# Norm and token shift in two parts behind the first MLP, and the weights' low parts there by VectorE, in a two-layer backbone

## What is computed

```python
def rms_norm(x, g, eps=NORM_EPS):
    xf = x.astype(jnp.float32)
    y = xf * lax.rsqrt(jnp.mean(xf * xf, axis=-1, keepdims=True) + eps)
    return (y * g.astype(jnp.float32)).astype(x.dtype)

def modulate(u, shift, scale):
    return u * (1 + scale) + shift

def sq_relu_mlp(u, w_up, w_down):
    return jnp.square(jax.nn.relu(u @ w_up)) @ w_down

def centred_shift(u):
    prev = jnp.pad(u[:, :-1], ((0, 0), (1, 0), (0, 0)))
    nxt = jnp.pad(u[:, 1:], ((0, 0), (0, 1), (0, 0)))
    return 0.5 * (prev + nxt)

# in rwkv_side, for the context and for the latent tokens apart:
    xx = centred_shift(u) - u
    mix = lambda i: u + xx * mu[i]
    xw, xk, xv, xa = mix(1), mix(2), mix(3), mix(4)
    k = xk @ w_rkv[1]
    v = xv @ w_rkv[2]
```

## Time and profile before

| | |
|---|---|
| median of three runs | 2558.79 us (2558.71 to 2562.51) |
| the profiled execution's own time | 2559.15 us |
| its span | 2557.4 us |
| TensorE busy | 2312.6 us, 90% |
| VectorE, ScalarE, GpSimd busy | 43%, 35%, 29% |
| mean granted clock of TensorE | 0.967 |

### The profile page before, as it was taken

How to read it: one execution, slowest core, us unless ns; L and a number is a source line. 1 busy time by engine, 2 the same in 40 slices (tenths; PEclk the granted TensorE clock), 3 DMA queues, 4 the chain that set the end, 5 groups by cost and what they waited for, 6 DMA issues and landing times.

```text
span 2557.4 us, 65184 instructions
## 1 busy us (share of the span) xinstructions
PE 2312.6 (90%) x27579; PEld 1915.4 (75%) x27579; DVE 1103.1 (43%) x2374; ACT 900.8 (35%) x1581; POOL 736.9 (29%) x531
## 2 busy tenths in 40 slices
PE   5998899999999999789978888888988868899998
PEld 3776677888888888668846777777777757888887
DVE  2326666351111212253354666666666644511113
ACT  3555555342121212222223344244244213522324
POOL 0334555232222222353302121121121112344442
PEclk9999999999999999889989999999999978999999
DMA  7125555112222112113410000000000002233321
GB/s 243 50 50 162 169 175 157 50 50 66 66 66 66 66 49 66 49 58 116 136 45 23 12 14 23 12 15 22 12 14 23 4 19 83 83 99 98 98 82 67
DMA packets 172312, 176.31 MB, mean 69 GB/s; under 512 B 26512, under 2 KB 160032, under 8 KB 172064
## 3 DMA queue, kind: packets, MB, share of 16 engines
q1 hardware_dynamic: 172064, 172.62, 21.4%
HBM read 161.06 MB, written 11.53 MB: 67 GB/s over the span
## 4 chain that ended last, share of the span: by engine, by line
PE 81%; DVE 9%; issue 4%; ACT 3%; POOL 1%; DMA 1%; SPq 0%; ACTq 0%; DVEq 0%; PEldq 0%
PE PS L385 39%; PE PS L1386 5%; PE PS L554 4%; PE PS L405 3%; PE PS L738 2%; PE PS L1371 2%; PE PS L1497 2%; PE PS L719 2%; PE PS L1192 2%; PE PS L1361 2%; PE PS L698 2%; PE PS L728 1%; PE PS L1476 1%; PE PS L1046 1%; PE PS L1488 1%
## 5 line engine op out<-in xcount | busy, mean ns | idle before, releaser
L365 POOL TENSOR_TENSOR WL<-RAW,WH 128x1024 fp32r<-128x1024 f32 x178 | 427.6, 2424 | 938.7 <-ACT WH L352 895.6
L385 PE MATMUL PS<-AH,WH 128*128 128x512 f32 (+1 forms) x1024 | 363.8, 355 | 6.2 <-DVE AL L2178 2.4
L385 PE MATMUL PS<-AH,WL 128*128 128x512 f32 (+1 forms) x1024 | 364.2, 356 | 0.0
L385 PE MATMUL PS<-AL,WH 128*128 128x512 f32 (+1 forms) x1024 | 361.6, 353 | 0.0
L352 ACT ACTIVATE WH<-RAW 128x1024 fp32r<-128x1024 f32 x172 | 171.9, 1047 | 271.4 <-PE PS L385 265.7
L385 PE MATMUL PS<-BH,WL 128*128 128x256 f32 (+1 forms) x736 | 261.0, 355 | 0.0
L385 PE MATMUL PS<-BH,WH 128*128 128x256 f32 (+1 forms) x736 | 260.1, 353 | 0.0
L385 PE MATMUL PS<-BL,WH 128*128 128x256 f32 (+1 forms) x736 | 259.0, 352 | 0.0
L661 DVE SCALAR_TENSOR_TENSOR X<-PS,MOD,X 128x256 f32 (+3 forms) x104 | 62.0, 653 | 379.4 <-PE PS L385 379.4
L385 PEld LDWEIGHTS PS<-AH,WH 128*128 128x128 f32 x1024 | 193.8, 189 | 36.4 <-issue 4.7
L385 PEld LDWEIGHTS PS<-AL,WH 128*128 128x128 f32 x1024 | 193.0, 188 | 28.5
(11 more groups left out here) (259 smaller groups left out, 4740.9 us busy)
## 6 DMA issues: line engine op xcount, KB each, us to landing
ADW<-l_ada_w SPq DMA_DIRECT2D x40, 1024.0 KB, 5.3
RAW<-l_mlp_up SPq DMA_DIRECT2D x64, 512.0 KB, 4.3
RAW<-l_mlp_down SPq DMA_DIRECT2D x64, 512.0 KB, 4.0
RAW<-l_w_rkv SPq DMA_DIRECT2D x24, 512.0 KB, 4.7
rwkv_scratch<-STG SPq DMA_DIRECT2D x24, 384.0 KB, 3.2
ADA<-l_ada_w SPq DMA_DIRECT2D x4, 2048.0 KB, 16.6
RAW<-l_w_in SPq DMA_DIRECT2D x16, 256.0 KB, 5.7
RAW<-l_w_out SPq DMA_DIRECT2D x16, 256.0 KB, 5.1
```

The source lines that it names most:

```text
L365: e.tensor_tensor(WL[:, s, rows], RAW[:, s, rows], WH[:, s, rows], ALU.subtract).then_inc(w_split[h], 1)
L385: mm = e.matmul(dst, w[:, s, k, n * P:(n + 1) * P], r[:, k, lo:hi], start=(k == 0 and i == 0), stop=(k == KT - 1 and i == 2), skip_group_c ...
```

## The change

1. **Norm 2 and the token shift in two parts**, context and latents. The last two units of the MLP compute the context's columns first, and the first two units behind the shift too; their latent columns are computed for two units at once, as before.
2. **The first mix in another form**: MX = (mu / 2) (previous + next) + (1 - mu) U. ScalarE makes the scaled row MV = (1 - mu) U and copies the two edges; VectorE sums the neighbours and makes MX in one step. XX = 0.5 XX - U, which the later mixes need, is made behind the second part (`shift_rest`). GpSimd has no step of the shift left. Two small VectorE steps at the start make the rows (1 - mu) and mu / 2.
3. **Low parts by VectorE** (`low_half`) for the first two units behind norms 1, 2 and 3, between other steps; GpSimd skips these six units. ScalarE splits at other blocks (`SPLIT_AT`).
4. The matmuls behind a norm no longer wait for the evacuation of the two units before (`evacuated=False`); the PSUM columns of a part are laid so that they are free (`part_ps`). The sums for the norm stand at other k of the product.
5. In the last norm the transposes of the first half are issued two k later, in other banks.

The core of the diff (counters that only follow from it are left out):

```diff
+        def low_half(e, u, s, h):
+
+            rows = slice(4 * h, 4 * h + 4)
+            e.wait_ge(w_high[h], u + 1)
+            e.tensor_tensor(WL[:, s, rows], RAW[:, s, rows], WH[:, s, rows], ALU.subtract).then_inc(w_split[h], 1)
...
-        PARTS = (((CTX, LATENTS),), ((CTX,), (LATENTS,)), ((CTX, LATENTS),), ((FIRST,), (SECOND,)), ((FIRST,), (SECOND,)))
+        PARTS = (((CTX, LATENTS),), ((CTX,), (LATENTS,)), ((CTX,), (LATENTS,)), ((FIRST,), (SECOND,)), ((FIRST,), (SECOND,)))
...
-            pe_part(e, u, 0, rh, rl, b, b[0], k_ready=k_ready, behind=sums_after(i, 0, 3), done=w_used)
-            pe_part(e, u + 1, 1, rh, rl, b, b[0], k_ready=k_ready, behind=behind, done=w_used)
+                pe_part(e, u + n, n, rh, rl, a, part_ps(i, 0), k_ready=k_ready, done=in_done)
+            pe_part(e, u, 0, rh, rl, b, part_ps(i, 1), k_ready=k_ready, behind=sums_after(i, 0, 0 if i < 3 else 2), done=w_used)
+            pe_part(e, u + 1, 1, rh, rl, b, part_ps(i, 1), k_ready=k_ready, behind=behind, done=w_used)
...
+            for n in range(2):
+                pe_part(e, u + n, n, AH, AL, a, a[0], k_ready=after_norm(i, 0),
+                        behind=sums_after(i, 1, sums[1]) if n == sums[0] else None, evacuated=False)
+            for n in range(2):
+                pe_part(e, u + n, n, AH, AL, b, b[0], k_ready=after_norm(i, 1), done=w_used, evacuated=False)
...
+        SPLIT_AT = {1: (6, 7), 3: (1, 4)}
...
+            for j in (2, 3):
+                add_part(e, i, 0, u - 4 + j, j % 2, 2 * j, layer, chunk)
+                norm_dve_squares(e, i, j, 0)
+            norm_dve(e, i, layer, half, 0, behind=split_behind)
+            add_part(e, i, 1, u - 2, 0, 4, layer, chunk)
+            norm_dve_squares(e, i, 2, 1)
+            add_part(e, i, 1, u - 1, 1, 6, layer, chunk)
+            low_half(e, u + 1, 1, 0)
+            norm_dve_squares(e, i, 3, 1)
+            low_half(e, u + 1, 1, 1)
+            norm_dve(e, i, layer, half, 1)
...
+                    e.activation(XX[:, i, edge], TN[:, i % 2, beside], ACT.Identity, bias=bias)
+                    e.activation(U[:, i, a0:a1], TN[:, i % 2, a0:a1], ACT.Identity, bias=bias).then_inc(n_h, 1)
+                    if i >= 2:
+                        e.wait_ge(mx_made, KT * p + i - 1)
+                    e.wait_ge(n_h, at)
+                    e.activation(MV[:, i % 2, a0:a1], U[:, i, a0:a1], ACT.Copy, scale=MU1[:, i:i + 1]).then_inc(xx_step, 1)
+                if i >= 1:
+                    k = i - 1
+                    e.wait_ge(mx_made, KT * p + k + 1)
+                    e.activation(AH[:, k, a0:a1], MX[:, k % 2, a0:a1], ACT.Copy).then_inc(mx_high, 1)
...
+            scaled(0)
+            for k in range(KT + 1):
+                if k + 1 < KT:
+                    scaled(k + 1)
+                if k < KT:
+                    e.wait_ge(n_h, high + k + 1)
+                    e.tensor_tensor(XX[:, k, a0 + 1:a1 - 1], U[:, k, a0:a1 - 2], U[:, k, a0 + 2:a1], ALU.add)\
+                     .then_inc(xx_ready, 1)
...
+                    e.scalar_tensor_tensor(out=MX[:, k % 2, a0:a1], in0=XX[:, k, a0:a1], scalar=MU2[:, k:k + 1],
+                                           in1=MV[:, k % 2, a0:a1], op0=ALU.mult, op1=ALU.add).then_inc(mx_made, 1)
+                if k >= 1:
+                    e.wait_ge(mx_high, mixed + k)
+                    e.tensor_tensor(AL[:, k - 1, a0:a1], MX[:, (k - 1) % 2, a0:a1], AH[:, k - 1, a0:a1],
+                                    ALU.subtract).then_inc(mx_low, 1)
+                    if behind is not None:
+                        behind(k - 1)
...
+            shift_act(e, 0, range(0, 5))
+            split_half(e, u, 0, LANDED[u], 0)
+            shift_act(e, 0, range(5, 6))
+            norm_act_squares(e, 2, 2, u - 2, 1)
+            split_half(e, u, 0, LANDED[u], 1)
+            shift_act(e, 0, range(6, KT + 1))
+            e.sem_inc(evac_act, 1)
+            split_half(e, u + 1, 1, LANDED[u + 1], 0)
+            norm_act_squares(e, 2, 3, u - 1, 1)
+            split_half(e, u + 1, 1, LANDED[u + 1], 1)
+            norm_act_stats(e, 2, 1)
+            shift_act(e, 1, range(KT + 1))
...
+            shift_dve(e, 0, behind=between)
+            norm_dve_squares(e, 2, 2, 1)
+            add_part(e, 2, 1, u - 1, 1, 6, 0, 5)
+            low_half(e, u + 1, 1, 0)
+            norm_dve_squares(e, 2, 3, 1)
+            low_half(e, u + 1, 1, 1)
+            shift_dve(e, 1)
+            shift_rest(e)
...
-            pe_behind_norm(pe, 1, U_MLP0, 5)
+            pe_behind_norm(pe, 1, U_MLP0, (0, KT - 1))
...
-            pe_behind_norm(pe, 3, U_MLP1, KT - 1)
+            pe_behind_norm(pe, 3, U_MLP1, (1, 4))
...
             def first_half(e, k):
+                if k >= 2:
+                    final_block(0, k - 2)
```

More of the change, by code:

```diff
@@ L501, in norm_act_high, with norm_dve @@
                 ins.then_inc(n_h, 1)
-        def norm_dve(e, i, layer, half, p):
+        def norm_dve(e, i, layer, half, p, behind=None):
             if p == 0:
@@ L596, in act_around_norm @@
             norm_act_stats(e, i, 0)
-            norm_act_high(e, i, layer, half, 0, range(0, 2))
-            split_half(e, u, 0, LANDED[u], 0)
-            norm_act_high(e, i, layer, half, 0, range(2, 5))
-            split_half(e, u, 0, LANDED[u], 1)
-            norm_act_high(e, i, layer, half, 0, range(5, KT))
+            for k in range(KT):
+                norm_act_high(e, i, layer, half, 0, range(k, k + 1))
+                if k in SPLIT_AT[i]:
+                    split_half(e, u, 0, LANDED[u], SPLIT_AT[i].index(k))
             e.sem_inc(evac_act, 1)
@@ L960, in shift_pe, with around_edge, shift_act @@
-        def shift_pe(e):
-            e.wait_ge(w_split[0], U_RKV + 3)
-            e.wait_ge(evac_act, U_RKV + 2)
-            e.wait_ge(evac_dve, U_RKV + 2)
+        def around_edge(part):
+            a0, a1, _ = part
+            return slice(a0, a1, a1 - a0 - 1), slice(a0 + 1, a1 - 1, a1 - a0 - 3)
+        def shift_act(e, p, blocks):
+            part = PARTS[2][p][0]
+            a0, a1, st = part
+            edge, beside = around_edge(part)
+            e.wait_ge(par_ready, 5)
+            for i in blocks:
+                if i < KT:
+                    at = TN_AT[2] + KT * p + i + 1
+                    bias = MOD[:, 1, i, 1 - st:2 - st]
+                    e.wait_ge(n_t, at)
+                    e.activation(XX[:, i, edge], TN[:, i % 2, beside], ACT.Identity, bias=bias)
[8 more added lines that the diff above has]
+                    e.activation(AH[:, k, a0:a1], MX[:, k % 2, a0:a1], ACT.Copy).then_inc(mx_high, 1)
@@ new lines, in dve_around_shift, with between @@
+        def dve_around_shift(e, u):
+            def between(k):
+                if k == 4:
+                    low_half(e, u, 0, 0)
+                    add_part(e, 2, 1, u - 2, 0, 4, 0, 5)
+                if k == 5:
+                    low_half(e, u, 0, 1)
+            for j in (2, 3):
+                add_part(e, 2, 0, u - 4 + j, j % 2, 2 * j, 0, 5)
+                norm_dve_squares(e, 2, j, 0)
+            shift_dve(e, 0, behind=between)
[6 more added lines that the diff above has]
+            shift_rest(e)
@@ L1799, in _ @@
             slots(pool, pool_pre, pool_inverse, pool_chain)
-            with pool.Fori(U_OUT1 // 2, UNITS // 2) as i:
+            for u in range(U_OUT1, U_MLP1):
+                pool_split(pool, u, u % 2)
+            with pool.Fori(U_MLP1 // 2 + 1, UNITS // 2) as i:
                 for s in range(2):
@@ L2193, in _ @@
             mlp0_up(3)
[L2194 removed]
+            for j in range(2):
                 add_dve(dve, U_RKV - 4 + j, j % 2, 2 * j, 0, 5, 0, (2, j))
[L2197 to L2198 removed]
+            dve_around_shift(dve, U_RKV)
             for j in range(12):
```

194 lines of the change are left out of this document (90 added, 104 removed).

## The result

The changed kernel took 2529.49 us (median of four runs, 2524.67 to 2532.1) beside 2559.97 for the kernel before (four runs): a ratio of 0.9878, 95% interval 0.986 to 0.9895. The forecast was 2530.0, with a range of 2522 to 2543: the kernel is faster, as forecast, and the time lies within the range. The profiled execution took 2524.67 us, its span is 2522.9 at a mean granted clock of 0.975.

The account below looks back on a forecast made before the run. TensorE was taken as the bound, with time to gain only where it stands or runs at the lower clock. Gains of 4.4 + 21.0 + 3.7 + 0 = 29.1 from 2559.15 gave 2530.0 us, range 2522 to 2543.

Parts of the forecast that it names:

- Place A: The norm behind attention: earlier sums and no wait for evacuation, gain 4.4 us, bounds 3 and 5.3.
- Place B: Norm and token shift behind the first MLP: done in two parts, gain 21.0 us, bounds 11 and 23.5.
- Context blocks: First part of the shift behind the first MLP: four VectorE steps, 1.8 us per block with hand-offs.
- Latent blocks: Second part of the shift behind the first MLP: VectorE sets the pace at 2.75 us per block.
- Clock: Shift behind the first MLP: TensorE's waits may bring the lower clock level once, 1.5 us added.
- Table load: ScalarE's load before the norm's exponential costs its 1.28 us and no drain besides.
- Place C: The norm of the second layer: no wait for evacuation, shorter waits for low parts, gain 3.7 us, bounds 2 and 4.5.
- Place D: The end, last norm: transposes two k later move nothing, gain 0, bounds -0.6 and +0.5.
- hand-offs: Rival at the two-part shift: full step times and 0.1 us per hand-off, 2540 us; chance 0.16.
- No clock cost and a pitch of 2.6: Rival at the two-part shift: TensorE's waits cost no clock, VectorE's pitch is 2.6, 2526 us; chance 0.11 with more.
- The lower clock ending slower: Rival: the lower clock stays through both parts behind TensorE's waits in Place B and Place C, 2566 us; chance 0.02.
- That the parts don't do what they say: Rival: TensorE still waits for a GpSimd split or evacuation at Place B, 11.6 us more, 2541.6; chance 0.06.

Follow-up runs that it names:

- run 9: Changed kernel with 26 extra matmuls, their products unread, in TensorE's wait for the first latent block of the shift; Place B took 78.16 us.
- Run 3: Changed kernel with the first mix in its old form, in two parts, without the scaled row by ScalarE; Place B took 85.81 us.
- run 2: Changed kernel with the low parts behind norms 1, 2 and 3 by GpSimd again; 2532.1 us, ratio 0.9885 to the kernel before.
- run 6: Changed kernel with matmuls behind norms 1, 2 and 3 waiting for the evacuation again; 2525.22 us, Place C took 57.96 us.
- run 7: Changed kernel with the last norm's transposes right behind their block again, changed banks kept; Place D took 41.11 us.
- run 5: The changed kernel once more with no edit; Place A 70.45, Place B 78.13, Place C 52.84, Place D 42.12 us.

## Why the prediction was right, and where it was off

**Place A**: forecast 4.4, measured 4.54. The sums came behind one k with a wait of 0.63 us for VectorE (0.9 forecast), and nothing waited behind them.

**Place B**: forecast 21.0, measured 24.56, with the end at 1117.0 - 1035.2 = 81.8 us behind its start, where it was 78.15. The steps, as distances from the start of B:

| step | forecast | measured |
|---|---|---|
| first scaling | 17.9 | 17.8 |
| sixth low block | 36.8 | 34.7 |
| scaling of the latents | 49.0 | 46.8 |
| first latent block at TensorE | 54.9 | 52.9 |
| next unit | 81.8 | 78.15 |

- *Context blocks*: the first scaling was right to 0.1. The term that was mis-sized is the way to the sixth block: 1.58 us per block, not 1.8 (0.9 over four blocks); VectorE's waits for ScalarE's split at the fifth were 0.4, not 0.7; and ScalarE's squares begin behind the first of two additions (1057.49, the addition from 1056.72), not behind both (0.7). That is 1.9 of the 2.1 us; the later steps up to the first latent block kept it. Of the two waits of TensorE that the sum had there, 2.4 us for a low half and 0.8 for the sums, the first did not come and the second was 0.42.
- *Latent blocks*: 2.75 us forecast, VectorE did one in 2.65. The number was nearly right for the wrong engine: from the third block TensorE's 2.73 is the bound (run 9). Run 3 shows VectorE as the bound, at 3.38. The last low block at 1107.3 is not 1090.1 + 7 x 2.75 = 1109.3; the prediction doesn't say why, but the last blocks have no scaling between them and came closer: 16.0 us for the seven steps, not 7 x 2.65 = 18.6.
- *Clock*: the prediction added 1.5 us for one fall to the lower level. The fall came (0.61 from 1079 to 1083 us) and cost nothing here, since with the clock at 1.00 the place took as long (run 9). This term was added without asking whether TensorE would have waited in that stretch anyway. With the 2.1 us above this is the 3.6 us that B was better than forecast.
- *Table load*: the exponential of the second part starts 0.01 us behind the 1.28 us load, and the load 0.02 behind the logarithm, so no drain. The Trainium skill, page "ScalarE: Activation LUTs", section "What ACT_TABLE_LOAD costs", gives about 1380 ns of drain besides. The trace doesn't agree, and the sum by the row was right to leave it out.
- *ScalarE's edge copies*: 0.28 to 0.30 us where 0.20 was taken. ScalarE kept up all the same.

**Place C**: forecast 3.7, measured 3.96. The wait for the low half was 1.32 us, not 2.2, the one for the first block 1.89, as forecast 1.9. Runs 2 and 6 show what carries it: both edits are needed. The prediction had counted the lower level behind the old wait (7.71 us for 5.8 of work) into the gain, and run 6 bears that out.

**Place D**: forecast 0 with -0.6 as the bound, measured -1.15 and -1.09. The term was mis-sized: the prediction let the last addition hide the delay. By run 7 and the runs with the delay it costs 0.6, and another 0.5 where the sums fall to the lower level.

**Sum**: forecast 29.1, measured 31.9 in the four places. From 2559.15 that would have been 2527.2; the median of the four runs, 2529.49, lies nearer to the forecast than the working deserves, since the recurrence alone took between 1013.3 and 1020.8 us in these profiles.

**Rivals**: hand-offs (2540) fell, the pitch was shorter than forecast. No clock cost and a pitch of 2.6 (2526) is nearest to what the stretches show (2527.2), though the clock did fall. The lower clock ending slower fell: the level came back 3.2 us behind the first latent matmul. Its sum was also loose: 2207.9 with 17.4 us doubled is 2225, not 2222, which would make its price 2569 and not 2566; nothing of the forecast rests on it. That the parts don't do what they say fell too: place B would then be 11.6 us longer than forecast, and it is 3.6 shorter.

What varies in the recurrence from one execution to the next was not followed. One idea wasn't tried: with no two k between the two units of the latents, TensorE would have twelve matmuls for each block from the first on. An estimate by run 5, whose first latent matmul starts at 1082.5 us: 1082.5 + 8 x 2.73 = 1104.3 for the end of the last, in place of 1107.1, if the granted clock is 1.00 from the start.

## What to carry to other kernels

When several places change at once, cut the span at one engine's marks and compare stretches: here A, B and C repeat within 0.2 us where whole times of one kernel differ by 7. Before paying for an engine's clock or pitch, ask whether it would wait in that stretch anyway: the lower level cost nothing in place B (run 9) and some 2.2 us in place C (run 6). And before moving work off VectorE to GpSimd, or behind something, look at what runs beside it there.
